# Where the weights' high and low parts lie in on-chip memory: slots 64 bytes longer, low parts 64 bytes further on

## The chip, the cores and the metric

The kernel is one program on one core of a Trainium2 chip. A core has TensorE (matmuls, called PE in the profile, with the loading of its stationary operand shown apart as PEld), VectorE (DVE), ScalarE (ACT), GpSimd (POOL) and SyncE (SP), which here only issues the DMAs. The metric is the time of one execution in microseconds (us), the median of several; lower is better.

## The reference

Two layers of a decoder trunk over 512 tokens of width 1024. Everything that costs time is a product of activations with a weight matrix:

```
for l in range(2):
    h = h + 0.5 * swiglu(rms(h), ffn1_wi[l], ffn1_wo[l])        # 1024 -> 2 x 2816 -> 1024
    n = rms(h);  z = n @ w_in[l]                                # one wide projection
    y_a = conv_module(z_conv) @ conv_out[l]                     # causal depthwise conv, 31 taps
    y_b = spatial_gating(z_sgu) @ sgu_out[l]
    y_c = sparse_attention(z_q, z_kv, z_ngate) @ nsa_out[l]
    h = h + (g_a * y_a + g_b * y_b + g_c * y_c) @ w_out[l]
    h = h + cross_attention(rms(h), rms(mem), xq[l], xkv[l], xo[l])   # 256 memory tokens
    h = h + 0.5 * swiglu(rms(h), ffn2_wi[l], ffn2_wo[l])
```

All is float32.

## The kernel before

**Three products for one.** A float32 product is made of three matmuls on operands of the type fp32r. Each operand is split into a high part (a copy that ScalarE writes as fp32r) and a low part (what is left, a subtraction): high weights by high activations, high weights by low activations, low weights by high activations. All three add up in one PSUM bank.

**Units.** The weights go through the core in "units" of 128 columns. A full unit has 8 tiles of 128 x 128 (a contraction of 1024), so 24 matmuls of 512 columns; the short units (branch outputs, the third chunk of an FFN) have 4 or 6 tiles. There are 236 units in each layer, 472 in all. Each goes through a chain of slots in SBUF:

- SP (line 408 in most units) waits until the slot of `raw` is free and issues two DMAs from HBM into it. `raw` has 2 slots of 4096 bytes in each partition.
- ScalarE copies `raw` into a slot of `wH` (`split`, line 1274; the trace books it under the helper's line 1261) when the unit that used this slot four units ago is through its matmuls. It works 3 units ahead.
- GpSimd subtracts: `wL = raw - wH` (`low`, lines 655 and 656).
- TensorE waits for that and issues the unit's matmuls (`unit`, lines 706, 709 and 712).
- VectorE or ScalarE takes the result out of PSUM.

`wH` and `wL` have 4 slots each, chosen by the unit's number modulo 4. The lines that touch them:

```
wL[:, s % 4, 0:n, :] = raw[:, s % 2, 0:n, :] - wH[:, s % 4, 0:n, :]          # GpSimd, L655
mm(o, wH[:, s, k, :], rh(k));  mm(o, wH[:, s, k, :], rl(k));  mm(o, wL[:, s, k, :], rh(k))
```

In these matmuls the weight tile is the stationary operand (it is loaded into the array, 128 columns) and the activation tile `gxH`, `gxL`, `hH` or `hL` is the moving one (512 columns stream through). In `by_token` (line 733) the roles are exchanged: four tiles of `wH` or `wL` side by side are the 512 moving columns. That is so in 288 matmuls.

**Beside the weights.** GpSimd also computes one of the four column groups of the convolution, a tap at a time, between its subtractions: line 680 multiplies a window of `cin` (a part of `convb`) that starts 4 bytes further on with each tap, line 683 adds the product to a sum. VectorE computes the other three groups (line 1893) and most of the element-wise work of the FFNs (lines 1785 to 1794).

**Layout.** Tensors lie one behind the other in each partition in the order of their declarations: `raw` (8,192 bytes), `wH` (16,384), `wL` (16,384), `xT`, `gxH`, `gxL`, `hH`, `hL` and `big` (16,384 each), `convb` (16,864), `qT` and so on. So before the change all slots of `raw`, `wH` and `wL` are whole multiples of 4096 bytes apart, and all tiles of the moving activations are multiples of 2048 bytes from them. The order of the work is written out by hand in one list for each engine, with semaphores between them; nothing in it depends on addresses.

Of the kernel before, what the change touches and what calls it, by code (L numbers as in the profile page):

```python
# [6 lines left out]
F32R = mybir.dt.float32r  # L7
# [5 lines left out]
P = 128  # L13
# [4 lines left out]
def trunk(nc, x, mem, norm_ffn1, ffn1_wi, ffn1_wo, norm_mix, w_in, conv_w, conv_b, conv_ln_g,  # L18
# [20 lines left out]
    KD = D // P  # L39
# [33 lines left out]
    with ctx:  # L73
        def sb(name, shape, dt=F32):
            return ctx.enter_context(nc.sbuf_tensor(name, shape, dt))


        raw = sb("raw", [P, 2, KD, P])
        wH = sb("wH", [P, 4, KD, P], F32R)
        wL = sb("wL", [P, 4, KD, P], F32R)  # L80
        xT = sb("xT", [P, KD, T])
        gxH = sb("gxH", [P, KD, T], F32R)
        gxL = sb("gxL", [P, KD, T], F32R)
# [2312 lines left out]
```

## Time and profile before

| | |
|---|---|
| median of 3 runs | 2674.22 us (2672.18 to 2682.71) |
| profiled execution | span of 2674.3 us from first to last instruction, which is its own time |
| TensorE busy by the page | 98% of the span |
| GpSimd, VectorE, ScalarE busy | 46%, 53%, 41% |
| granted TensorE clock, mean | 0.997 of full speed |

Matmuls are pipelined: the duration that the trace gives one (0.39 us for 512 columns) is its passage through the array, and the next begins before it ends. What a matmul costs is therefore the distance from one start to the next, to be read from a timeline, and not its duration. A busy share near 100% does not tell whether this distance is as short as it can be.

### The profile page before, as it was taken

How to read it: one execution, taken by the hardware profiler on the slowest of the kernel's cores; microseconds unless marked ns; L12 is line 12 of the kernel's file. 1: busy time of each engine (PE TensorE's matmuls, PEld its weight loads, DVE VectorE, ACT ScalarE, POOL GpSimd, SP SyncE). 2: the span in 40 equal slices, each digit the busy share in tenths (PEclk: the TensorE clock that was granted, in tenths of full speed). 3: DMA queues.
4: the chain of work that ended last, by engine and by line, in shares of the span. 5: the costliest groups of instructions: out<-in, count | busy, mean ns of one | idle time of the engine just before them, and what ended most of it. 6: DMA issues, size and time to landing. Idle time of an engine off the chain costs nothing.

```text
span 2674.3 us, 35749 instructions
## 1 busy us (share of the span) xinstructions
PE 2633.2 (98%) x12597; PEld 2110.3 (79%) x12597; DVE 1404.5 (53%) x1813; ACT 1095.5 (41%) x1674; POOL 1230.6 (46%) x616
## 2 busy tenths in 40 slices
PE   8999999999999999999999999999999999999999
PEld 6888878866778778888888888887667787788887
DVE  4343458966536544252553535698664364543433
ACT  5322242367644554222342222424675445532222
POOL 4443446762234334444444444477522353444443
PEclk9999999999999999999999999999999999999999
DMA  4334334322233223333333343333222332233332
GB/s 136 102 94 118 102 93 111 75 60 56 60 87 107 79 79 110 95 94 100 89 102 95 95 123 93 105 103 72 60 54 54 99 112 74 87 102 95 100 97 79
DMA packets 474694, 243.75 MB, mean 91 GB/s; under 512 B 41052, under 2 KB 466886, under 8 KB 474566
## 3 DMA queue, kind: packets, MB, share of 16 engines
q1 hardware_dynamic: 474542, 242.04, 32.1%
q8 instruction: 80, 1.31, 0.2%
q14 instruction: 48, 0.39, 0.0%
q10 hardware_dynamic: 24, 0.01, 0.0%
HBM read 237.79 MB, written 2.10 MB: 90 GB/s over the span
## 4 chain that ended last, share of the span: by engine, by line
PE 63%; issue 17%; POOL 9%; DVE 4%; POOLq 3%; ACT 3%; DMA 1%; DVEq 0%; ACTq 0%; SPq 0%
PE pg L706 19%; PE pg L709 18%; PE pg L712 18%; POOL wL L655 8%; PE pA L1003 1%; POOLq L682 1%; PE pA L828 1%; PE pA L950 1%; POOLq L684 1%; PE pg L733 1%; DVE convb L1893 1%; ACT wH L1261 1%; PE pg L1224 1%; PE pg L1222 1%; PE pg L1223 1%
## 5 line engine op out<-in xcount | busy, mean ns | idle before, releaser
L655 POOL TENSOR_TENSOR wL<-raw,wH 128x1024 fp32r<-128x1024 f32 (+1 forms) x472 | 1088.4, 2307 | 1410.2 <-ACT wH L1261 1406.5
L1261 ACT ACTIVATE wH<-raw 128x1024 fp32r<-128x1024 f32 (+1 forms) x472 | 477.6, 1012 | 1124.3 <-PE pg L712 962.5
L706 PE MATMUL pg<-gxH,wH 128*128 128x512 f32 (+1 forms) x2288 | 895.8, 392 | 1.0 <-DVE gxL L1743 0.5
L712 PE MATMUL pg<-gxH,wL 128*128 128x512 f32 (+1 forms) x2288 | 892.2, 390 | 0.0
L709 PE MATMUL pg<-gxL,wH 128*128 128x512 f32 (+1 forms) x2288 | 887.0, 388 | 0.0
L706 PEld LDWEIGHTS pg<-gxH,wH 128*128 128x128 f32 x2288 | 429.9, 188 | 100.2 <-issue 14.7
L712 PEld LDWEIGHTS pg<-gxH,wL 128*128 128x128 f32 x2288 | 429.9, 188 | 89.9 <-issue 4.4
L709 PEld LDWEIGHTS pg<-gxL,wH 128*128 128x128 f32 x2288 | 430.0, 188 | 87.1 <-issue 3.5
L706 PE MATMUL pg<-hH,wH 128*128 128x512 f32 x1008 | 400.0, 397 | 3.1 <-DVE hL L1794 3.1
L712 PE MATMUL pg<-hH,wL 128*128 128x512 f32 x1008 | 399.5, 396 | 0.0
L709 PE MATMUL pg<-hL,wH 128*128 128x512 f32 x1008 | 397.1, 394 | 0.0
L1775 DVE SCALAR_TENSOR_TENSOR xT<-pg,xT 128x512 f32<-128x512 f32 x112 | 77.2, 691 | 358.9 <-PE pg L712 358.6
L1787 DVE TENSOR_TENSOR tmp<-tmp,rstd 128x512 f32<-128x512 f32 x88 | 194.5, 2211 | 117.9 <-ACT tmp L1335 117.9
L1794 DVE TENSOR_TENSOR hL<-tmp,hH 128x512 f32 x88 | 190.2, 2161 | 90.6 <-ACT hH L1261 90.6
L709 PEld LDWEIGHTS pg<-hL,wH 128*128 128x128 f32 x1008 | 189.8, 188 | 51.0 <-issue 12.7
L706 PEld LDWEIGHTS pg<-hH,wH 128*128 128x128 f32 x1008 | 190.4, 189 | 43.0 <-DVE hL L1794 4.8
L712 PEld LDWEIGHTS pg<-hH,wL 128*128 128x128 f32 x1008 | 190.1, 189 | 36.3
L1785 DVE TENSOR_TENSOR tb<-pg,rstd 128x512 f32<-128x512 f32 x88 | 60.7, 690 | 125.4 <-PE pg L712 124.8
L1893 DVE SCALAR_TENSOR_TENSOR pA<-convb,par,pA 128x512 f32<-128x512 f32 x158 | 114.3, 752 | 7.4 <-issue 0.8
L1790 DVE TENSOR_TENSOR tmp<-pg,tmp 128x512 f32<-128x512 f32 x88 | 60.9, 692 | 100.0 <-PE pg L712 97.3
L1261 ACT ACTIVATE sq<-pA 128x512 f32<-128x512 f32 (+1 forms) x112 | 59.1, 528 | 101.4 <-PE pA L828 70.7
L683 POOL TENSOR_TENSOR convb<-convb,wsn 128x512 f32<-128x512 f32 x60 | 84.6, 1411 | 9.1 <-issue 0.4
(271 smaller groups left out, 2232.4 us busy)
## 6 DMA issues: line engine op xcount, KB each, us to landing
raw<-in_ffn_wi SPq DMA_DIRECT2D x352, 256.0 KB, 3.1
raw<-in_w_in SPq DMA_DIRECT2D x200, 256.0 KB, 3.3
raw<-in_ffn_wo SPq DMA_DIRECT2D x128, 256.0 KB, 3.0
raw<-in_ffn_wo SPq DMA_DIRECT2D x64, 192.0 KB, 2.5
raw<-in_xkv SPq DMA_DIRECT2D x32, 256.0 KB, 2.9
raw<-in_w_out SPq DMA_DIRECT2D x32, 256.0 KB, 3.0
raw<-in_sgu_out SPq DMA_DIRECT2D x32, 128.0 KB, 2.3
raw<-in_conv_out SPq DMA_DIRECT2D x32, 128.0 KB, 2.3
```

What stands on the lines that cost most here:

```text
L655: pool.tensor_tensor(wL[:, s % 4, 0:n, :], raw[:, s % 2, 0:n, :], wH[:, s % 4, 0:n, :].bitcast(F32), ALU.subtract)\
L683: pool.tensor_tensor(o, o, term, ALU.add)
L706: mm(o, wH[:, s, k, :], rh(k), start=(k == 0), stop=False)
L709: mm(o, wH[:, s, k, :], rl(k), start=False, stop=False)
L712: last = mm(o, wL[:, s, k, :], rh(k), start=False, stop=(k == kt - 1))
L1261: return act.activation(o, i, ACT.Copy, **kw)
L1775: STT(xT[:, k, :], bank, by, xT[:, k, :], ALU.mult, ALU.add).then_inc(evac, 1)
L1785: TTt(tb[:, 0, :], bank, rstd[:, :], ALU.mult).then_inc(evac, 1)
L1787: TTt(sr, sil, rstd[:, :], ALU.mult)
L1790: TTt(hb, bank, sr, ALU.mult).then_inc(evac, 1)
L1794: TTt(hL[:, slot, :].rearrange(flat), hb, hH[:, slot, :].rearrange(flat).bitcast(F32), ALU.subtract).then_inc(hid_l, 1)
L1893: STT(to, cin[:, j, k:k + T], w, o, ALU.mult, ALU.add)
```

## The change

The tensors `wH` and `wL` become views of longer ones, whose slots have 16 float32 (64 bytes) more than the 4096 bytes in use:

```
-        wH = sb("wH", [P, 4, KD, P], F32R)
-        wL = sb("wL", [P, 4, KD, P], F32R)
+        SLOT_WIDTH = KD * P + 16
+        wH_slots = sb("wH_slots", [P, 4, SLOT_WIDTH], F32R)
+        wL_slots = sb("wL_slots", [P, 4, SLOT_WIDTH], F32R)
+        wH = wH_slots[:, :, 0:KD * P].rearrange("p s (k c) -> p s k c", k=KD)
+        wL = wL_slots[:, :, 16:KD * P + 16].rearrange("p s (k c) -> p s k c", k=KD)
```

Slot s of `wH` now starts 64 s bytes behind the multiple of 4096 at which it was. `wL_slots` starts 256 bytes later than `wL` did, and its views 64 bytes further on, so slot s of `wL` is 320 + 64 s bytes behind its old multiple. All tensors declared after them lie 512 bytes further on. Inside a slot nothing changes: the 1024 elements that a copy or a subtraction touches still lie in one run, and so do the 128 of a weight tile. Every engine's list of instructions is the same as before, in the same order, with the same shapes and the same waits; only addresses differ. The 3 lines that the diff adds move all later line numbers by 3.

## Rows read from the trace of the kernel before

**Rows 1.** The page: span, and busy time, share and instructions by engine.

```profile
span 2674.3 us, 35749 instructions
PE 2633.2 (98%) x12597; PEld 2110.3 (79%) x12597; DVE 1404.5 (53%) x1813; ACT 1095.5 (41%) x1674; POOL 1230.6 (46%) x616
```

**Rows 2.** Timeline of PE alone, 1460 to 1500 us: start, duration, instruction.

```profile
1459.80 0.39 PE L709 MATMUL pg<-hL,wH 128*128 128x512 f32 x1
1460.03 0.39 PE L712 MATMUL pg<-hH,wL 128*128 128x512 f32 x1
...
1499.92 0.39 PE L709 MATMUL pg<-gxL,wH 128*128 128x512 f32 x1
```

**Rows 3.** By stretch: busy us (x instructions) of PE, PEld, DVE, ACT, POOL; clock; DMA.

```profile
1460.00:1500.00 40.00, 40.00 (x178) 33.11 (x177) 14.59 (x12) 9.62 (x12) 16.78 (x7) 1.00 0.33 95
400.00:500.00 100.00, 100.00 (x502) 81.32 (x501) 90.07 (x106) 35.77 (x46) 69.12 (x43) 1.00 0.37 98
500.00:600.00 100.00, 97.39 (x530) 73.21 (x529) 75.52 (x128) 47.63 (x95) 73.57 (x52) 1.00 0.26 66
```

**Rows 4.** Groups of instructions by line and shape, POOL, ACT and PE.

```profile
L655 POOL TENSOR_TENSOR wL<-raw,wH 128x1024 fp32r<-128x1024 f32 x420 | 1018.4, 2426 | 1315.9 <-ACT wH L1261 1313.2 <-issue 0.5
L655 POOL TENSOR_TENSOR wL<-raw,wH 128x512 fp32r<-128x512 f32 x52 | 70.3, 1351 | 94.3 <-ACT wH L1261 93.3
L683 POOL TENSOR_TENSOR convb<-convb,wsn 128x512 f32<-128x512 f32 x60 | 84.6, 1411 | 9.1 <-issue 0.4
L1261 ACT ACTIVATE wH<-raw 128x1024 fp32r<-128x1024 f32 x420 | 444.9, 1060 | 1088.4 <-PE pg L712 953.2 <-DMA raw<-in_ffn_wi 55.3 <-DMA raw<-in_w_in 31.5
L706 PE MATMUL pg<-gxH,wH 128*128 128x512 f32 x2224 | 877.3, 394 | 1.0 <-DVE gxL L1743 0.5 <-DVE gxL L1829 0.3
L706 PE MATMUL pg<-hH,wH 128*128 128x512 f32 x1008 | 400.0, 397 | 3.1 <-DVE hL L1794 3.1
L733 PE MATMUL pg<-wH,gxH 128*128 128x512 f32 x96 | 40.0, 417 | 0.0
```

**Rows 5.** Timeline, 111 to 116 us, GpSimd's subtraction beside the matmuls.

```profile
110.98 2.39 POOL L655 TENSOR_TENSOR wL<-raw,wH 128x1024 fp32r<-128x1024 f32 x1 [3.11 <-ACT wH L1261]
...
111.18 0.39 PE L706 MATMUL pg<-hH,wH 128*128 128x512 f32 x1
...
113.22 0.39 PE L706 MATMUL pg<-hH,wH 128*128 128x512 f32 x1
...
115.71 0.39 PE L712 MATMUL pg<-hH,wL 128*128 128x512 f32 x1
```

**Rows 6.** Timeline of TensorE, around 846 us, 256 columns.

```profile
846.13 0.28 PE L709 MATMUL pg<-gxL,wH 128*128 128x256 f32 x1
...
846.97 0.28 PE L712 MATMUL pg<-gxH,wL 128*128 128x256 f32 x1
```

**Rows 7.** Timeline of weight loading alone, 564 to 565 us.

```profile
564.64 0.19 PEld L709 LDWEIGHTS pg<-gxL,wH 128*128 128x128 f32 x1
564.75 0.19 PEld L712 LDWEIGHTS pg<-gxH,wL 128*128 128x128 f32 x1
```

**Rows 8.** Line 733 (weights as the moving operand), timeline from 475 us.

```profile
475.67 0.39 PE L733 MATMUL pg<-wH,gxL 128*128 128x512 f32 x1
...
477.94 0.39 PE L733 MATMUL pg<-wL,gxH 128*128 128x512 f32 x1
```

**Rows 9.** One line: the convolution's windows, durations in ns (min/median/max).

```profile
L680 POOL TENSOR_SCALAR wsn<-convb,par x60: 684/698/2181, 427.1 to 1898.1; 128x512 f32<-128x512 f32 x60
```

**Rows 10.** Busy time by stretch of the instructions of line 655 alone.

```profile
400.00:500.00 100.00, 41.84 (x18) 1.00 0.37 98
500.00:600.00 100.00, 31.88 (x16) 1.00 0.26 66
```

**Rows 11.** Who waited for whom: total us, times, longest.

```profile
POOL wL L655 <- ACT wH L1261: 1406.5, 430, 11.3
ACT wH L1261 <- PE pg L712: 962.5, 279, 4.8
```

## The prediction

> **What bounds the kernel now.** I read the page first. TensorE is busy for 98% of a span of 2674.3 us, the three engines that prepare its work for 41 to 53% [rows 1]. But a busy share says nothing about the pace, since matmuls overlap. So the second view is the timeline of TensorE alone in a calm stretch of an FFN. The first start shown is 1459.80 and the last 1499.92; the same stretch holds 178 matmuls [rows 2, 3], so 177 steps took 40.12 us, 226.67 ns each, with no gap anywhere. The granted clock is 1.00 there, the upper of the two levels, 2.4 GHz [rows 3]. 512 columns at 2.4 GHz are 213.33 ns, so each matmul costs 13.3 ns more than its columns. That surplus is the one place where the kernel's bound could hide something that depends on addresses, and the case turns on it.
>
> Third, who waits. GpSimd waits 1406.5 us in all for ScalarE's copy, and ScalarE 962.5 us for TensorE to free a slot of `wH` [rows 11]. A slot is refilled as soon as TensorE is through with it, and the new high and low parts then lie ready for about three units. Of a full unit's 24 x 0.2267 = 5.44 us the copy takes 1.06 and the subtraction about 2.4 [rows 4, 5]. The engines that write and read these slots are thus early, and TensorE sets the end.
>
> **The change, part by part.** It removes and adds no instruction and no wait. The lists of all five engines are the same; only addresses move. So the sum has a term for each kind of access to `wH` and `wL`, and each is number of accesses times what an access gains or loses by its address.
>
> *The stationary reads (lines 706, 709, 712).* 3 x (2224 + 1008) = 9696 of 512 columns [rows 4]. If slots at equal offsets clashed between the engines that use them at once, matmuls would be spaced wider while GpSimd reads `raw` and `wH` and writes `wL`. From 111.18 to 113.22 GpSimd's subtraction runs (110.98 to 113.37) and 9 steps take 2.04 us, 226.7 ns each; from 113.22 to 115.71, nearly all of it with GpSimd idle, 11 steps take 2.49 us, 226.4 ns each [rows 5]. GpSimd beside the matmuls costs them 0.3 ns a step at most. The mean says the same: GpSimd is busy for 16.78 and ScalarE for 9.62 of the 40 us in which all 177 steps make 226.67 [rows 2, 3]. A gain from TensorE keeping out of the way of the writers is therefore nothing, at most 9696 x 0.3 ns = 3 us. A loss is bounded by the cover: two loads of weights, one from `wH` and one from `wL`, start 0.11 us apart [rows 7] where nothing holds them back, and one is needed every 0.2267 us. A load could take twice as long and still be hidden. Term: 0.
>
> *The moving reads (line 733).* 3 x 96 = 288 matmuls [rows 4] that stream from `wH` or `wL`, with no cover. Today 10 steps take 2.27 us, 227 ns each, the same as with an activation as the moving operand [rows 8]. The trace has no weight tile at an odd offset. From below the bound is nothing; from above I take a tenth of the columns' time, since the nearest rows (below) show no effect at all: 288 x 21 ns = 6 us. I take 0.
>
> *GpSimd's subtraction (line 655).* 420 of 1024 elements at 2.426 us, 52 of 512 at 1.351 [rows 4]. Before, its three streams are whole multiples of 4096 bytes apart; after, slot 0 of `wH` stays so with `raw`, the others do not. The nearest row is line 683: also two inputs and one output of 512 elements, on tensors that are not multiples of 4096 apart, at a mean of 1.411 us against 1.351 for the subtraction of 512 [rows 4]. And line 680 reads a window that moves by 4 bytes with each tap: its minimum and median over 60 are 684 and 698 ns [rows 9], so no offset stands out. I take 0. Were the subtraction faster by any amount, GpSimd would only wait longer.
>
> *ScalarE's copy (line 1261).* 1060 ns for 1024 elements, and mostly idle before it, for TensorE [rows 4]. Same argument: 0.
>
> *The 512 bytes by which everything else moves.* All later tensors keep their distances to each other. 0.
>
> Sum: 2674.3 + 0 = 2674.3 us by the profiled execution, which stands within 0.1 us of the median, 2674.22. **I predict 2674 us.**
>
> The Trainium skill, "SBUF — State Buffer", section "Who interferes with whom", says that only the port pair that VectorE and GpSimd share causes contention, and that TensorE and ScalarE wait for nobody; by it the sum is the same. But another page of it speaks for the change. "TensorE: Matmul & The Clock Gate", section "Back-to-back issue gap", gives N/2.4 + 2.5 ns for the warm gap, 215.8 ns for 512 columns. The trace disagrees: 226.67 here, so by that rule 10.9 ns a matmul are in excess, and an estimate from it makes 9984 x 10.9 ns = 109 us and 2565 us if the excess were a clash that the offsets end.
>
> **Rivals.** *The surplus is a clash of equal offsets, and it goes (faster).* Weights start at multiples of 512 bytes from the activations in every matmul of the kind, so no row here has the two otherwise. Price: (9696 + 288) x 13.3 ns = 133 us, giving 2541 us. Against it: the surplus does not change with the distance inside that pattern, since tile k of the weights is 512 k bytes and tile k of the activations 2048 k bytes on, and 177 steps in a row still average 226.67 [rows 2, 3]. With 256 columns the step is 7 steps in 0.84 us, 120 ns [rows 6], 13.3 above the columns' 106.7, so the surplus goes with the instruction and not with the length of the stream. And with the roles exchanged it stays [rows 8]. It looks like a fixed cost of each matmul with its load. Half of it would suffice for 66 us. I give this 0.03, and another 0.03 to a gain of over 13 us by something I do not see.
>
> *GpSimd's subtraction gets slower and becomes the bound (slower).* The place is the projection and mixer stretch, 400 to 600 us and again in layer 2, where GpSimd also does the convolution. Of 69.12 busy us in the first hundred 41.84 are line 655, of 73.57 in the second 31.88 [rows 3, 10]. It decides from the point where the stretch is full: (100 - 27.28) / 41.84 = 1.74 times today's duration in the first, (100 - 41.69) / 31.88 = 1.83 in the second. At twice today's, 111.0 and 105.4 us of work would have to fit in 100 each, 16.4 us a layer, 33 in all: 2707 us. In the FFNs 4.8 us still fit in a unit's 5.44. Against it stand lines 683 and 680. 0.04.
>
> *The change does nothing that can be measured* is the forecast itself; it moves the offsets as it says, only not where anything looks at them. A mild loss in the moving reads (6 us) stays inside it. 0.88. The last 0.02 are for a loss of over 13 us that I do not see.
>
> **How the numbers follow.** A measurement of this kernel can tell about 0.5%, 13.4 us, from no change. Faster by more: 0.06. Within: 0.88. Slower by more: 0.06. The range takes in the bounds of the terms, 3 us down and 6 us up, and the spread of the runs shown, 2672.18 to 2682.71: 2668 to 2683 us. Both rivals lie outside it, and together with the unseen cases they hold 0.12.
>
> **What the profile of the changed kernel would show.** Right: the same calm stretch again has 226.67 ns from start to start; line 655 again takes 2.43 us in the mean and ScalarE's copy 1.06; line 733 again steps by 227 ns; GpSimd's wait for ScalarE is near 1406 us. If the surplus was a clash, the step falls towards 213 ns, and ScalarE's wait for TensorE shrinks with it. If the subtraction slows, its mean rises above 4 us and TensorE's loads of weights begin to wait for line 655 between 400 and 600 us. Slots tell them apart within one profile: slot 0 of `wH` keeps its distance to `raw`, slot 3 of `wL` (320 + 192 = 512 bytes on) is still a multiple of 512 from it. An effect that shows in all slots alike is not the offset's. What would make me wrong is an access whose cost depends on the address, at the one spot without a sample in this trace: an fp32r weight tile off a multiple of 512 bytes from its activations.

## The result, and the profile after

The changed kernel takes 2719.86 us (2714.95 to 2722.84, 4 runs) against 2674.91 us for the kernel before (4 runs): 1.0159 times as long, 95% interval 1.0146 to 1.0172 (the ratio goes by all the runs; the quotient of the two medians is 1.0168). That is 45 us slower, where no change was forecast and 2683 us was the upper end of the range. The profiled execution has a span of 2717.7 us, 43.4 more than before.

The page, the lines that answer to [rows 1], and two of its groups (busy us, mean ns, then idle time and who ended it):

```profile
span 2717.7 us, 35749 instructions
PE 2675.9 (98%) x12597; PEld 2113.6 (78%) x12597; DVE 1411.2 (52%) x1813; ACT 1096.0 (40%) x1674; POOL 1234.0 (45%) x616
L658 POOL TENSOR_TENSOR wL_slots<-raw,wH_slots 128x1024 fp32r<-128x1024 f32 (+1 forms) x472 | 1092.8, 2316 | 1449.8 <-ACT wH_slots L1264 1446.4
L1264 ACT ACTIVATE wH_slots<-raw 128x1024 fp32r<-128x1024 f32 (+1 forms) x472 | 477.1, 1011 | 1155.9 <-PE pg L715 1001.6
```

TensorE is busy for 42.7 us more, and the others do the same work in nearly the same time: GpSimd 1234.0 us against 1230.6, ScalarE 1096.0 against 1095.5, VectorE 1411.2 against 1404.5. GpSimd's wait for ScalarE and ScalarE's for TensorE have each grown by some 40 us, as they must when TensorE is slower [rows 11]. So neither the copies nor the subtractions, but the pace of the matmuls changed. The timeline of PE alone in the calm stretch, to be read against [rows 2]:

```profile
1459.65 0.39 PE L715 MATMUL pg<-hH,wL_slots 128*128 128x512 f32 x1
1459.88 0.40 PE L709 MATMUL pg<-hH,wH_slots 128*128 128x512 f32 x1
1460.11 0.39 PE L712 MATMUL pg<-hL,wH_slots 128*128 128x512 f32 x1
1460.34 0.39 PE L715 MATMUL pg<-hH,wL_slots 128*128 128x512 f32 x1
...
1499.90 0.40 PE L715 MATMUL pg<-gxH,wL_slots 128*128 128x512 f32 x1
```

And the busy time by stretch (PE, PEld, DVE, ACT, POOL; clock; DMA):

```profile
1460.00:1500.00 40.00, 40.00 (x175) 32.50 (x174) 4.84 (x7) 7.43 (x7) 17.10 (x8) 1.00 0.31 92
```

175 matmuls start from 1459.65 to 1499.90, so 174 steps took 40.25 us: 231.3 ns each, against 226.67, at the same clock of 1.00 and with no idle moment. Over the whole trace I took all steps under 260 ns between matmuls of 512 columns in lines 706 to 712 (709 to 715 after): some 9,100 in either trace, with a mean of 227.19 ns before and 231.22 after. The difference of 4.03 ns by the 9696 matmuls of 512 columns in these lines is 39 us of the 43.4.

The steps are also no longer alike. Before, the calm stretch repeats 227, 226 and 227 ns for the three matmuls of a triple, in all slots and tiles alike (from the starts in the trace). After, slot 0 has 228, 229 and 236 ns for the three of a triple, slot 1 has 236, 228 and 229, and in slots 2 and 3 the steps range from 224 to 241 from tile to tile, repeated in the next unit that uses the slot. With the same instructions in the same order in all units of this stretch, a pattern that repeats with the slot points to addresses.

### The profile page after: what moved, and what is told of

Same layout as the page of the kernel before. It is cut to its first block, busy times and chain, and to the rows that moved or that the text cites. A ratio compares the mean times of both kernels' runs of the same rounds, so it can differ in the third digit from the quotient of the medians.

```text
span 2717.7 us, 35749 instructions
## 1 busy us (share of the span) xinstructions
PE 2675.9 (98%) x12597; PEld 2113.6 (78%) x12597; DVE 1411.2 (52%) x1813; ACT 1096.0 (40%) x1674; POOL 1234.0 (45%) x616
## 4 chain that ended last, share of the span: by engine, by line
PE 67%; issue 16%; POOL 8%; DVE 5%; ACT 3%; DVEq 1%; DMA 0%; POOLq 0%; ACTq 0%; SPq 0%
PE pg L709 20%; PE pg L715 19%; PE pg L712 19%; POOL wL_slots L658 8%; PE pg L736 2%; PE pA L831 1%; PE pA L1006 1%; PE pA L953 1%; DVE convb L1896 1%; PE pg L1225 1%; PE pg L1227 1%; PE pg L1226 1%; PE pA L1164 1%; ACT wH_slots L1264 1%; DVE sacc L1756 0%
## 5 line engine op out<-in xcount | busy, mean ns | idle before, releaser
L658 POOL TENSOR_TENSOR wL_slots<-raw,wH_slots 128x1024 fp32r<-128x1024 f32 (+1 forms) x472 | 1092.8, 2316 | 1449.8 <-ACT wH_slots L1264 1446.4
L1264 ACT ACTIVATE wH_slots<-raw 128x1024 fp32r<-128x1024 f32 (+1 forms) x472 | 477.1, 1011 | 1155.9 <-PE pg L715 1001.6
L709 PE MATMUL pg<-gxH,wH_slots 128*128 128x512 f32 (+1 forms) x2288 | 906.1, 396 | 2.2 <-DVE big L1963 1.1
L715 PE MATMUL pg<-gxH,wL_slots 128*128 128x512 f32 (+1 forms) x2288 | 901.1, 394 | 0.0
L712 PE MATMUL pg<-gxL,wH_slots 128*128 128x512 f32 (+1 forms) x2288 | 892.9, 390 | 0.0
L709 PEld LDWEIGHTS pg<-gxH,wH_slots 128*128 128x128 f32 x2288 | 430.0, 188 | 107.7 <-issue 14.1
L715 PEld LDWEIGHTS pg<-gxH,wL_slots 128*128 128x128 f32 x2288 | 430.2, 188 | 99.8 <-issue 4.4
L712 PEld LDWEIGHTS pg<-gxL,wH_slots 128*128 128x128 f32 x2288 | 430.5, 188 | 95.8 <-issue 3.5
L709 PE MATMUL pg<-hH,wH_slots 128*128 128x512 f32 x1008 | 404.5, 401 | 2.8 <-DVE hL L1797 2.8
L715 PE MATMUL pg<-hH,wL_slots 128*128 128x512 f32 x1008 | 403.9, 401 | 0.0
```

The lines of the kernel that those rows point to most:

```text
L658: pool.tensor_tensor(wL[:, s % 4, 0:n, :], raw[:, s % 2, 0:n, :], wH[:, s % 4, 0:n, :].bitcast(F32), ALU.subtract)\
L709: mm(o, wH[:, s, k, :], rh(k), start=(k == 0), stop=False)
L712: mm(o, wH[:, s, k, :], rl(k), start=False, stop=False)
L715: last = mm(o, wL[:, s, k, :], rh(k), start=False, stop=(k == kt - 1))
L1264: return act.activation(o, i, ACT.Copy, **kw)
```

## Experiments

Theory A: what TensorE reads for the load of a weight tile clashes with its stream of activations, and how much goes by the offset between the two. Rival B: slots at unlike offsets upset the engines that fill them. Rival C: only the low parts' 64 bytes cost. Rival D: what counts is where a tile itself starts, not its distance to another.

Spacing below is measured like that above: the first and last start in the calm stretch from 1460 to 1500 us and the number of steps between, or a stretch of the probe. Ratios are to the kernel before, with 95% intervals. Each probe (1, 5, 7 and 9) was executed once.

**1. TensorE alone, one offset after another.** This kernel computes nothing of the reference. ScalarE first fills the tensors, then TensorE runs the stretches with no other engine at work.

```
for name in w:                       # wa, wb, ... differ only in their offset
    for j in range(240):
        k = j % 8
        pe.matmul(pg[:, j // 24 % 4, :], w[name][:, k * P:(k + 1) * P], mov[:, k % 4, :], ...)
```

> A kernel that computes nothing of the reference: TensorE alone, 16 stretches of 240 matmuls of 512 fp32r columns, each with its own 128x128 weight tile loaded, no other engine at work meanwhile. Only the offset of the weights' tensor from a multiple of 4096 bytes behind the moving tensor differs: 0 (wa), 4 (wb), 16 (wc), 32 (wd), 64 (we), 96 (wf), 128 (wg), 192 (wh), 256 (wi), 320 (wj), 384 (wk), 448 (wl), 512 (wm), 1024 (wn), 2048 (wo), 0 again (wp). Theory A (the load of a weight tile and the stream of activations clash inside TensorE's own reads, by their offsets): spacing 226.7 ns at 0, 512, 1024 and 2048, and other values, 228 to 236 or also below 226, at the rest. Rival B (the clash is with ScalarE and GpSimd, which write and read other slots): 226.7 ns or less in all 16 stretches alike.

The rows of single tiles (durations min/median/max in ns, first and last start in us; 239 steps lie between):

```profile
L66 PE MATMUL pg<-mov,wb x240: 388/392/399, 78.3 to 133.8; 128*128 128x512 f32 x120
L66 PE MATMUL pg<-mov,wc x240: 389/389/397, 134.0 to 188.2; 128*128 128x512 f32 x120
L66 PE MATMUL pg<-mov,we x240: 393/396/398, 244.4 to 300.2; 128*128 128x512 f32 x120
L66 PE MATMUL pg<-mov,wg x240: 390/393/404, 356.7 to 412.2; 128*128 128x512 f32 x120
L66 PE MATMUL pg<-mov,wh x240: 388/392/397, 412.4 to 467.1; 128*128 128x512 f32 x120
L66 PE MATMUL pg<-mov,wi x240: 388/389/395, 467.4 to 521.6; 128*128 128x512 f32 x120
L66 PE MATMUL pg<-mov,wj x240: 390/396/398, 521.8 to 577.5; 128*128 128x512 f32 x120
L66 PE MATMUL pg<-mov,wk x240: 388/393/404, 577.8 to 633.3; 128*128 128x512 f32 x120
L66 PE MATMUL pg<-mov,wl x240: 388/392/394, 633.5 to 688.2; 128*128 128x512 f32 x120
L66 PE MATMUL pg<-mov,wp x240: 388/389/389, 851.7 to 905.8; 128*128 128x512 f32 x120
```

Offset 0 (wp): 54.1 / 239 = 226.4 ns, by the nanoseconds in the trace 226.67. Offset 4 (wb): 232.4. 16 (wc): 226.7. 64 (we): 233.3. 128 (wg): 232.4. 192 (wh): 228.9. 256 (wi): 226.7. 320 (wj), 384 (wk) and 448 (wl) repeat 64, 128 and 192 with 233.3, 232.4 and 228.9; 512, 1024 and 2048 give 226.67. So the offset matters in TensorE alone, as theory A says, and the kernel before sat on the lowest value. Two offsets missed what was expected of them: 16 and 256 were to differ from 226.7 ns and did not, and the period of 256 bytes was read off only here. Rival B is not needed for the effect, since no other engine ran; whether it adds something in the kernel is for the next experiments.

**2. The two halves of the edit.** First the longer slots without the shift of the low parts (the diff is against the full edit):

```
-        wL = wL_slots[:, :, 16:KD * P + 16].rearrange("p s (k c) -> p s k c", k=KD)
+        wL = wL_slots[:, :, 0:KD * P].rearrange("p s (k c) -> p s k c", k=KD)
```

> The slots 64 bytes longer, but the low parts not 64 bytes further on: wH slot s at 64 s, wL slot s at 256 + 64 s. Theory A: the pace is set by pairs of offsets, so most of the 45 us come back in another mixture, slot by slot, 2690 to 2725 us; slot 0 of wH with wL at 256 differs from slot 3 at 192 and 448. Rival B (slots that differ among themselves upset ScalarE and GpSimd): 2720 us, all slots alike in their spacing of matmuls. Rival C (only the 64 bytes of the low parts cost): 2675 us.

2715.38 us, 1.0148 (1.0129 to 1.0167). 175 steps in 40.31 us: 230.3 ns. In this kernel the high and the low parts of a slot lie at one offset modulo 256: 0 in slot 0, 64, 128 and 192 in the others. So each slot should have the pace that the probe has at its offset. Here are the first and last start of 19 steps inside a unit of slot 0 and of 21 steps inside the next one, of slot 1:

```profile
1473.54 0.39 PE L709 MATMUL pg<-hH,wH_slots 128*128 128x512 f32 x1
...
1477.85 0.39 PE L712 MATMUL pg<-hL,wH_slots 128*128 128x512 f32 x1
...
1479.00 0.39 PE L709 MATMUL pg<-hH,wH_slots 128*128 128x512 f32 x1
...
1483.90 0.39 PE L709 MATMUL pg<-hH,wH_slots 128*128 128x512 f32 x1
```

That is 4.31 us / 19 and 4.90 us / 21. By the nanoseconds in the trace, inside the units of the four slots between 1440 and 1540 us, the steps are 226.67, 233.3, 231.9 and 228.9 ns, and the probe has 226.67, 233.3, 232.4 and 228.9 at 0, 64, 128 and 192. The probe's four values average to 230.3 ns, which is the pace measured above.

Then the shift of the low parts alone, slots of 4096 bytes (against the kernel before):

```
-        wL = sb("wL", [P, 4, KD, P], F32R)
+        wL_slots = sb("wL_slots", [P, 4 * KD * P + 128], F32R)
+        wL = wL_slots[:, 16:4 * KD * P + 16].rearrange("p (s k c) -> p s k c", s=4, k=KD)
```

> Slots of 4096 bytes as before, the low parts 64 bytes further on and nothing else: high parts at 0 to the activations in every slot, low parts at 64. Theory A: the same spacing pattern in all four slots, not 226.67 in all three matmuls of a triple; 2690 to 2725 us. Rival C: 2720 us, all of the loss. Rival B (it takes slots with unlike offsets): 2675 us.

2712.17 us, 1.0137 (1.0117 to 1.0157); 231.1 ns, with 228, 229 and 236 in the triple of all four slots, the pattern that the full edit has in slot 0. Each half alone costs most of the whole (38 and 35 us of 45), so the costs of the halves do not add. Rival C fails by the first kernel, B by the second.

**3. The other side moved instead.**

```
         wL = sb("wL", [P, 4, KD, P], F32R)
+        sb("gap", [P, 16])
```

> Weights where they were before, 64 bytes of nothing behind them, so that the activations (and all later tensors) lie 64 bytes further on. Theory A (the offset between the two that TensorE reads at once counts): every pair is at -64 bytes, so the spacing changes from 226.67 in all slots alike, to a time other than 2675 us by over 13 us, either way. Rival D (the weight tile's own start counts, a multiple of 512 plus the same rest being good): 2675 us, since the weights have not moved.

2696.58 us, 1.0076 (1.0057 to 1.0095), 228.9 ns. The weights had not moved by a byte. The weights are then at -64, which is 192 modulo 256, and 228.9 ns is what the probe has at 192. Line 733, where the roles are exchanged, checks the sign: there the activations are stationary and lie at +64 from the weights that stream. Its median step is 233 ns, the probe's pace at 64, against 227 before.

**4. All of it moved, and the edit in steps of 256.** The line `sb("gap", [P, 16])` now stands ahead of `raw`:

> 64 bytes of nothing ahead of raw, so that raw, weights and activations all lie 64 bytes further on and keep their distances. Theory A: 2675 us and 226.67 ns. Rival D (a tile's own start counts): slower or faster by over 13 us.

2675.42 us, 1.0002 (0.9992 to 1.0011), 226.7 ns. And the full edit with another number (the diff is against the full edit):

```
-        SLOT_WIDTH = KD * P + 16
+        SLOT_WIDTH = KD * P + 64
-        wL = wL_slots[:, :, 16:KD * P + 16].rearrange("p s (k c) -> p s k c", k=KD)
+        wL = wL_slots[:, :, 64:KD * P + 64].rearrange("p s (k c) -> p s k c", k=KD)
```

> The whole edit, with 256 bytes in the place of 64: slots 256 bytes longer, low parts 256 bytes further on. Slots have different offsets modulo 4096 but the same modulo 256. Theory A with a period of 256 bytes: 2675 us, no change, 226.67 ns everywhere. Rival B (unlike slots cost) or any account by distances between slots: 2715 to 2720 us.

2675.52 us, 1.0004 (0.9992 to 1.0017), 226.7 ns. Together with 3 they show what counts: the offset between weights and activations modulo 256 bytes. It is not where either starts (all moved, and nothing changed) and not how the slots lie to each other (in 3 they lay as before, and the pace changed).

**5. Finer offsets, both moved, smaller loads and streams.** TensorE alone again; nothing of the reference is computed.

> TensorE alone again, 240 matmuls a stretch, nothing of the reference computed. First 13 stretches: offsets of the weights behind the moving tensor of 0 (wa), 8, 12, 20, 24, 48, 160, 176, 208, 224, 240, 252 and 64 (wm) bytes. Theory A with a period of 256 bytes, as the first probe suggests: 226.7 at 0, something between 226 and 235 at the others; whether any offset gives less than 226.67 is open, and I expect none does (the two offsets 0 and 16 gave the least so far). Then the moving tensor 64 bytes on as well (movb): theory A says 226.7 for weights at 64 (wm, both moved alike) and near 228.9 for weights at 0 (the offset is 192 modulo 256); theory D (the start of each by itself) says another than 226.7 for the first. Then 64 and 32 columns of weights instead of 128, at 0 and 64: if the clash costs by the length of the load, the surplus over 213.3 falls with it (13.3 to about 7 and 3 at offset 0); if it is a fixed cost of the switch, it stays 13.3. Then 256 moving columns: 120.0 at offset 0; at 64 between 113 and 127.

Offsets of 12, 20, 48, 160, 208 and 224 gave 233.3 ns, 8 gave 230.7, 24 gave 231.1, 176 gave 230.0, 240 and 252 gave 226.7. Weights and moving tensor both 64 on: 226.85, as theory A says and D does not. None is below 226.67. The smaller loads went against the guess in the text. The stretches hold, in order, 64 columns of weights at offsets 0 and 64, 32 columns at 0 and 64, and 128 columns of weights with only 256 moving ones at 0 and 64 (PE, PEld, ACT, POOL):

```profile
860.00:905.00 45.00, 45.00 (x198) 26.21 (x196) 0.00 (x0) 0.00 (x0) 1.00 0.00 1
915.00:960.00 45.00, 45.00 (x195) 26.13 (x194) 0.00 (x0) 0.00 (x0) 1.00 0.00 1
970.00:1015.00 45.00, 45.00 (x196) 21.16 (x195) 0.00 (x0) 0.00 (x0) 1.00 0.00 0
1025.00:1070.00 45.00, 45.00 (x196) 21.17 (x195) 0.00 (x0) 0.00 (x0) 1.00 0.00 0
1082.00:1102.00 20.00, 20.00 (x169) 20.00 (x168) 0.00 (x0) 0.00 (x0) 1.00 0.00 1
1108.00:1128.00 20.00, 20.00 (x179) 20.00 (x178) 0.00 (x0) 0.00 (x0) 1.00 0.00 1
```

By the starts, half and a quarter of a load cost more than a whole one at offset 0 (230.0 and 231.7 ns), and a little less at offset 64 (232.7 and 231.7 ns against 233.3). With 32 columns of weights the two offsets no longer differ. And with 256 moving columns the order turns round: 120.0 ns at offset 0, 113.3 at 64. So neither of these two offsets is the better one for every shape.

**6. Sixteen bytes.** As the low parts' shift in 2, with 4 elements instead of 16:

> As only_low_parts, with 16 bytes instead of 64. Theory A, with 226.67 ns at an offset of 16 in the probe: 2675 us. If mixing offsets within a triple is what costs (high parts at 0, low parts at another offset), 2690 us or more.

2712.23 us, 1.0137 (1.0113 to 1.0161): a miss, by 37 us. Then both parts shifted alike, `wH` and `wL` as views that begin 4 elements into their tensors:

> High and low parts both 16 bytes further on (low_parts_16 moved the low ones alone and lost 38 us). Theory A: a constant offset of 16 costs nothing, as in the probe, and what costs is that the offset changes within a triple: 2675 us and 226.67 ns. If an offset of 16 costs by itself in this kernel: 2710 us or more.

2717.3 us, 1.0148 (1.0122 to 1.0174), 233.3 ns: a second miss. So the mixture within a triple was not the reason. The stretches say more (columns as in [rows 3]), first two of `low_parts_16`, then two of the kernel with both parts moved:

```profile
1100.00:1200.00 100.00, 100.00 (x443) 82.81 (x442) 42.29 (x32) 26.91 (x32) 43.84 (x19) 1.00 0.34 100
1450.00:1550.00 100.00, 100.00 (x432) 80.85 (x431) 36.31 (x29) 24.28 (x28) 42.93 (x19) 1.00 0.33 95
```

```profile
1450.00:1550.00 100.00, 100.00 (x430) 81.00 (x429) 36.50 (x28) 24.29 (x28) 43.18 (x18) 1.00 0.32 94
2450.00:2550.00 100.00, 100.00 (x443) 82.80 (x442) 44.04 (x32) 26.11 (x32) 43.12 (x18) 1.00 0.33 97
```

All are calm FFN stretches with the same code, and within a kernel with the same offsets. In `low_parts_16` one has 443 matmuls in 100 us (226.7 ns, the pace of the kernel before), the other 432. With both parts at 16 it is 443 and 430 (233.3 ns). So the probe's 226.7 ns at 16 does occur in the kernel, from about 2,400 us on, and most of the earlier time has the slower pace. This offset has two steady paces, and the theory of the offset alone does not say which one comes.

**7. What comes before.** That was tried with TensorE alone (no part of the reference is computed), each offset four ways (the lines are cut out of the loop).

```
run(ps[2 * i], "we", 24)                          # 24 matmuls at offset 64
run(ps[2 * i], name, N).then_inc(gone, 1)         # pu, px: straight on
pe.wait_ge(back, pauses)                          # a copy on ScalarE
last = run(ps[2 * i + 1], name, N)                # pv, py: behind the pause
```

> TensorE alone, nothing of the reference computed; it asks why an offset of 16 bytes gave 226.67 ns in the first probe and near 233 in the kernel with both parts moved by 16. Offsets 0 (wa), 16 (wb), 12 (wc), 240 (wd), 64 (we) and 192 (wf), 192 matmuls a stretch. Each in four ways: a new tile for each matmul, straight behind 24 matmuls at offset 64 (output pu), the same behind a pause in which ScalarE copies once (pv), and the kernel's triple (high tile, high tile again with the other moving tile, low tile), straight on (px) and behind a pause (py). Theory A1 (what precedes decides which of several steady patterns a stretch falls into): pu and pv differ at 16, say 226.67 and 233.3, and at 0 they don't. Theory A2 (the triple decides): pu and pv are alike, px and py alike and near 233 at 16. At 0 all four give 226.67 by either, since the kernel before shows nothing else; at 64 all four near 233.

Single rows, 191 steps each (wc is 12 bytes, wf 192):

```profile
L76 PE MATMUL pu<-mov,wc x192: 394/394/397, 399.4 to 443.9; 128*128 128x512 f32 x192
L76 PE MATMUL pv<-mov,wc x192: 387/396/496, 445.1 to 489.1; 128*128 128x512 f32 x192
L76 PE MATMUL px<-mov,wf x192: 392/397/398, 1066.7 to 1111.2; 128*128 128x512 f32 x192
L76 PE MATMUL py<-mov,wf x192: 388/392/505, 1112.4 to 1156.2; 128*128 128x512 f32 x192
```

At 12 bytes 44.5 us straight on and 44.0 behind the pause, and without the first step, which takes in the restart, 233.3 and 230.0 ns; in the latter 236 and 224 alternate. At 192 in triples 44.5 and 43.8 us, 233.3 and 229.0 ns. So there are two paces at 12 and at 192 as well, and the stretch behind the pause has the faster one, though not in every way (at 12 in triples both have 233.3, at 192 with single tiles both have 228.9). That is in favour of A1, with two reserves. The stretches behind a pause also write to another PSUM tensor, which the probe does not separate from the pause. And at 16, where a difference was expected, all four ways gave 233.3, while the first probe had 226.7 behind a stretch at 4 bytes. Offset 240 is another such case: 226.7 in the second probe, 228.3 in all four ways here. Offset 0 gave 226.7 to 226.8 in all four, and 64 gave 233.3.

**8. A price foretold from the probe.** Activations 192 bytes further on, `sb("gap", [P, 48])` behind `wL`, so all weights at offset 64:

> Weights where they were, activations and all behind them 192 bytes further on, so that every weight tile is at 64 modulo 256 from its activations. Theory A with the first probe's row for 64 (233.34 ns in place of 226.67 in every matmul): 9984 x 6.67 ns = 67 us, 2741 us. If the probe's single tensors do not carry over to triples (the same high tile loaded twice, then the low one), another value, 2700 to 2750 us. If the weights' own start or the slots' distances counted, 2675 us.

2727.23 us, 1.0178 (1.0159 to 1.0198). The calm stretch has 172 steps in 40.13 us, 233.3 ns, as the probe. The loss is 50 us by the medians and not 67, so the pace was foretold and the sum was too high. Most of the difference is in what was multiplied. The mean step under 260 ns before was 227.2 ns and not 226.67, so it rises by 6.1 ns to 233.3. There are 9,107 such steps between matmuls of 512 columns and not 9984, and added up they take 56 us more, where the span grows by 53. The steps of 260 ns and more between such matmuls, mostly waits, do not grow (111.1 us in all against 112.6). The matmuls of 256 columns are faster at 64, but by 4.8 ns in the mean and not by the probe's 6.7, 0.9 us for 192. In line 733 the offset is the reverse, 192, and its median is 230 ns, near the probe's 228.9.

**9. A faster layout?** TensorE alone, nothing of the reference: tiles 0, 64, 128 or 192 bytes more than 512 apart, moving tiles 0 to 192 more than 2048.

> TensorE alone, nothing of the reference computed: 24 stretches of 240 matmuls of 512 columns. The weights' tiles lie 512 bytes apart and 0 (wa), 64 (wb), 128 (wc) or 192 (wd) more, the moving tiles 2048 bytes apart and 0 (ma), 64 (mb), 128 (mc), 192 (md), 32 (me) or 16 (mf) more, so the offset between the weight tile that is loaded and the tile that streams changes from matmul to matmul. Theory A: a stretch's spacing is some mean over its offsets, 226.67 for wa with ma and 229 to 235 for the rest, since no fixed offset gave less than 226.67. If the bytes between one moving tile and the next count by themselves (the next stream begins where the last left off), some stretches come out under 226.67, down to 220.0 (one step of 6.67 less), and a faster layout than both kernels' exists.

None of the 23 other stretches came under 228.3 ns (wc with mc, both 128 more); the rest lie from 230.0 to 235.0. No layout tried beats the kernel before, so none was built into it.

## Why the prediction was wrong

**The bound** was read rightly. TensorE's pace sets the time, and the pace was all that changed.

**The stationary reads** are the step that failed: "A load could take twice as long and still be hidden. Term: 0." That is an argument on how long a load takes, and the time in loads hardly changed: PEld is busy 2113.6 us against 2110.3. It was also weak by its own row, since the two loads that start 0.11 us apart in [rows 7] last 0.19 us each and overlap. What the runs show in its place is that the pace of the stream goes by the offset between the tile that is loaded and the tile that streams, and the stream is the path, so no cover hides it. The term measured 4.03 ns x 9696 = 39 us. (That the load holds up the stream, and not the stream the load, is how I read it; no run separates the two.) That GpSimd and ScalarE do not disturb the matmuls was right, but it answered another question.

**The surplus of 13.3 ns** was found and then called "a fixed cost of each matmul with its load". The arguments for that were weak in one way. Tiles at 512 k and 2048 k bytes, 256 columns, roles exchanged: all of these samples have offset 0 modulo 256, so their agreement said nothing of other offsets. The text named this spot at its end as the one without a sample, but gave it no price on the slow side, only a chance of 0.02 for a loss that it did not see.

**The first rival** had the right mechanism and the wrong sign. There is a cost that goes by offset inside TensorE's reads, yet equal offsets are its lowest point for 512 columns. The bound should have been drawn on both sides: a surplus that one does not understand can double as well as vanish. Plus and minus 13.3 ns x 9984 is 133 us either way. The worst offset measured, 234.3 ns (96 bytes), has 21.0 ns over the columns' 213.3.

**Two pages against the runs.** The Trainium skill, "SBUF — State Buffer", section "Who interferes with whom", says that TensorE waits for nobody and that only the port pair of VectorE and GpSimd is contended. As to other engines the runs agree: the probes reach the same paces alone. For TensorE itself that section lists two read ports, one for the moving operand and one for the load, as independent, and there the runs differ. The Trainium skill, "TensorE: Matmul & The Clock Gate", section "Step-by-step: what each phase is for", says that loading the next tile does not steal read bandwidth from the running matmul; here the measured pace depends on the offset between the two by up to 7.6 ns in 227, so the measurement decides. The gap of 215.8 ns, worked out from the Trainium skill's same page, section "Back-to-back issue gap", was reached by no layout tried. That section states its formula for the isolated gap of a single matmul, so it was no floor for this stream.

**The moving reads** of line 733 were put at 0 to 6 us. Their median rose from 227 to 232 ns and their mean (steps under 260 ns) from 228.6 to 231.8, about 1 us for 288; inside the bound. **GpSimd's subtraction** (2316 ns in the mean for both shapes, against 2307) and **ScalarE's copy** (1011 against 1012) were right, and the rival that rested on the subtraction did not come about.

**What stays open.** That the offset of the stationary tile against the moving one changes the pace is shown: by moving either side, both, by 256 bytes, and slot by slot in one kernel. It does not settle the pace alone, since 16, 12, 192 and 240 bytes have two. How the memory is built that makes it so, why 256 columns prefer the other offset and smaller loads cost more, and what chooses between two paces are not settled.

## What to carry to other kernels

A matmul stream without gaps need not be at its floor: take the distance of starts, subtract the columns at the granted clock, and ask what the rest depends on. If every sample in the trace shares a property, here offset 0 modulo 256 bytes between stationary and moving tile, their agreement is no evidence on it; price the case in which it is lost, on both sides. For fp32r tiles with 512 moving columns keep that offset at 0, and be wary of innocent padding or small new tensors between the weights and the activations: 64 bytes at one place cost 0.8% here.

## What was not expected of the hardware

- The pace of fp32r matmuls of 512 columns, each with its load, goes by the offset of the two in SBUF; the probe's values repeat after 256 bytes: 226.67 ns at 0, 228.9 at 192, 232.4 at 128, 233.3 at 64, 234.3 at 96, in TensorE alone.
- With 256 columns it is the reverse, of the two offsets tried: 120.0 ns at 0, 113.3 at 64.
- A load of 64 or 32 columns slows the stream more than one of 128 at offset 0 (230.0 and 231.7 ns), and with 32 columns offset 64 costs the same as 0.
- At some offsets there are two steady paces: 443 or 432 matmuls in 100 us in one kernel with the low parts at 16 bytes, 443 or 430 in one with both parts at 16. A pause before the stretch changed the pace at 12 and 192 bytes in TensorE alone, but not in every order of tiles.
